# First attention of a fused two-block kernel: scores with keys on partitions, split operands, sums from a product with ones

## What is computed

```
def mla_attention(q_nope, q_rope, k_nope, k_rope, v):
    ...
        s = (jnp.einsum('bqhd,bkhd->bhqk', qn_b, k_nope, preferred_element_type=jnp.float32)
             + jnp.einsum('bqhr,bkr->bhqk', qr_b, k_rope, preferred_element_type=jnp.float32))
        p = jax.nn.softmax(s * scale, axis=-1).astype(v.dtype)
        return jnp.einsum('bhqk,bkhd->bqhd', p, v)
...
        attn_l = mla_attention(qn_l, qr_l, k_nope, k_rope, v_all)
        four_l = fourier_mix(u_f, w_fourier[l])
        y_lat = jnp.concatenate([four_l, attn_l], axis=-1) @ w_out[l]
```

## Time and profile before

| | |
|---|---|
| median of three runs | 3804.72 us |
| the profiled execution, its own time | 3807.03 us |
| its span in the profile | 3805.2 us |
| PE busy | 3570.6 us, 94% |
| DVE busy | 1533.0 us, 40% |
| ACT busy | 1040.6 us, 27% |
| the chain that ended last | PE 86%, DVE 8%, ACT 3% |

### The profile page before, as it was taken

One profiled execution on the slowest core, in us unless ns is written; L12 is line 12 of the kernel. 1 busy time (PEld: TensorE's weight loads), 2 busy tenths in 40 slices (PEclk: granted clock), 3 DMA queues, 4 the chain that ended last, 5 costly groups with the idle time before them and its releaser, 6 DMA issues.

```text
span 3805.2 us, 42399 instructions
## 1 busy us (share of the span) xinstructions
PE 3570.6 (94%) x18350; PEld 2808.2 (74%) x18350; DVE 1533.0 (40%) x2253; ACT 1040.6 (27%) x1638; POOL 0.2 (0%) x4
## 2 busy tenths in 40 slices
PE   8978999899999999899998999778788999999997
PEld 7445666687888888788886678668673678888886
DVE  4324555453122223521112764555533452333334
ACT  2033333343211111411123542332321243112122
POOL 0000000000000000000000000000000000000000
PEclk9989999899999999999998899888899999999999
DMA  7300000131111111312332000000004331111112
GB/s 288 135 16 1 1 1 1 45 119 54 50 50 45 50 50 34 133 50 78 92 97 101 20 8 18 1 17 1 1 1 160 125 97 45 50 45 56 45 45 100
DMA packets 179881, 221.14 MB, mean 58 GB/s; under 512 B 5744, under 2 KB 135408, under 8 KB 176496
## 3 DMA queue, kind: packets, MB, share of 16 engines
q1 hardware_dynamic: 179696, 218.45, 17.3%
HBM read 185.92 MB, written 32.51 MB: 57 GB/s over the span
## 4 chain that ended last, share of the span: by engine, by line
PE 86%; DVE 8%; ACT 3%; issue 1%; DMA 1%; SPq 0%; DVEq 0%; ACTq 0%
PE ps L199 83%; PE ps L809 3%; DVE M L2150 1%; DMA wr<-in_w_down 1%; PE ps L237 1%; DVE ST L890 1%; DVE X L421 0%; DVE PT L849 0%; ACT SQJ L316 0%; DVE Yf L418 0%; PE ps L1853 0%; DVE Q L1185 0%; DVE RT L1184 0%; DVE S L886 0%; DVE Y L418 0%
## 5 line engine op out<-in xcount | busy, mean ns | idle before, releaser
L373 DVE TENSOR_TENSOR wl<-wr,wh 128x1024 fp32r<-128x1024 f32 x204 | 247.2, 1224 | 602.0 <-ACT wh L365 601.9
L199 PE MATMUL ps<-hTh,wh 128*128 128x512 f32 x1216 | 474.0, 390 | 5.4 <-DVE hTl L301 2.9
L199 PE MATMUL ps<-hTl,wh 128*128 128x512 f32 x1216 | 473.6, 389 | 0.0
L199 PE MATMUL ps<-hTh,wl 128*128 128x512 f32 x1216 | 473.6, 389 | 0.0
L365 ACT ACTIVATE wh<-wr 128x1024 fp32r<-128x1024 f32 x204 | 211.9, 1053 | 728.7 <-PE ps L199 489.6
L199 PE MATMUL ps<-wh,hidh 128*128 128x512 f32 x864 | 338.0, 391 | 8.7 <-DVE wl L373 8.7
L199 PE MATMUL ps<-wl,hidh 128*128 128x512 f32 x864 | 337.7, 391 | 0.0
L199 PE MATMUL ps<-wh,hidl 128*128 128x512 f32 x864 | 337.5, 391 | 0.0
L199 PE MATMUL ps<-M,M 128*128 128x128 f32 (+1 forms) x2176 | 276.7, 288 | 4.7 <-DVE M L2150 4.7
L199 PEld LDWEIGHTS ps<-M,M 128*128 128x128 f32 (+1 forms) x2176 | 259.9, 193 | 12.1 <-DVE M L2150 6.1
L199 PEld LDWEIGHTS ps<-hTh,wh 128*128 128x128 f32 x1216 | 228.6, 188 | 53.4 <-DVE hTl L301 3.3
(11 more groups left out here) (279 smaller groups left out, 4810.5 us busy)
## 6 DMA issues: line engine op xcount, KB each, us to landing
wr<-in_w_up SPq DMA_DIRECT2D x54, 512.0 KB, 4.0
wr<-in_w_down SPq DMA_DIRECT2D x54, 512.0 KB, 3.7
wr<-in_w_in SPq DMA_DIRECT2D x42, 512.0 KB, 4.5
late<-in_w_ada SPq DMA_DIRECT2D x16, 1024.0 KB, 5.4
wr<-in_w_out SPq DMA_DIRECT2D x32, 512.0 KB, 3.7
kept<-pb SPq DMA_DIRECT2D x30, 512.0 KB, 3.1
spill<-X SPq DMA_DIRECT2D x12, 1024.0 KB, 4.0
X<-spill SPq DMA_DIRECT2D x12, 1024.0 KB, 8.7
```

Source lines behind the costliest of these rows:

```text
L199: return e.op.matmul(out, left, right, start=start, stop=stop, skip_group_check=True)
L373: e.op.tensor_tensor(lo[:, 0:k * c], self.raw[n % 3][:, 0:k * c], hi[:, 0:k * c].bitcast(F32), ALU.subtract).then_inc(*e.event(self.name + ...
```

## The change

Scores are computed transposed: 128 keys on partitions, 512 queries as columns. So the exponential's output is already what the value product needs, and the ten transposes of P for each item and their copies are gone. A step is one key tile for one half of the queries of a head: 160 steps, 20 for each head. Each step has an `mm3` for the scores (bank n % 3), one exponential of 128 x 512 to E, a copy to the f32r tile Ph, the low part Pl = E - Ph on DVE, and an `mm3` with V, which adds up ten key tiles in a bank (5 or 6). Queries, keys and values are split in high and low f32r parts as well.

The row maximum can't be taken over partitions, so the high parts alone are multiplied once more with queries on partitions (24 chunks for each head, of 512, 512 and 256 keys, through banks 3 and 4), DVE takes maxima of these, and the negated maximum becomes row 96 of the queries, against a row of ones in the keys (97 rows in the contraction). That row is made by four small products with the identity and split as well ("row"). 64 columns of ones beside V give the sums, already spread over 64 partitions; after ten steps (a "unit") ACT copies sums and values out, and for two heads at a time DVE takes the reciprocal of 128 x 512 sums and multiplies; the quotient is split straight into cath and catl.

Side jobs (`JOBS`) for the next head stand at given steps: keys at 0, 1, 2, queries at 4 and 6, values at 7 and 8, chunks two at a time from 8 to 19, row 0 at 16 and row 1 at step 1 of the head itself. All side jobs share bank 7, and each waits on PE until the one before is read out of it. The first head's jobs run before the first step (n from -20). w_q is loaded after the projection stage. `FirstOut` has no transposes of O any more.

```diff
-        e.wait_ge(("read", group))
-        e.op.tensor_copy(self.Kh[1][64:96, :], self.Kh[0][64:96, :]).then_inc(*e.event("proj_dve", "kr_both"))
...
-    SIDE, PVB = 5, 7
...
+    SIDE, MAX, VALUE, STEPS = 7, 3, 5, 160
+    KEYS = (*HALVES, (1024, 1280))
+    JOBS = {0: [("k", 0)], 1: [("k", 1)], 2: [("k", 2)], 4: [("q", 0)], 6: [("q", 1)], 7: [("v", 0)], 8: [("v", 1)], 16: [("row", 0)]}
...
+        self.Q = [pair("Q", [128, 1024], (124 + 8 * i, 128 + 8 * i)) for i in range(2)]
+        self.K = [pair("K", [128, 1280], (182 + 10 * i, 187 + 10 * i)) for i in range(2)]
+        self.V = [pair("V", [128, 10, 128], (32 + 32 * i, 48 + 32 * i)) for i in range(2)]
+        self.E = [k.sb("E", [128, 512], o) for o in (153, 172)]
+        self.P = [pair("P", [128, 512], at) for at in ((174, 180), (176, 37), (178, 53))]
...
+    def jobs(self, n):
+        h, s = n // 20 + 1, n % 20
+        out = [("row", h - 1, 1)] if s == 1 and h > 0 else []
+        if h < 8:
+            out += [(what, h, i) for what, i in self.JOBS.get(s, [])]
+            if s >= 8:
+                out += [("max", h, m // 3, m % 3) for m in (2 * (s - 8), 2 * (s - 8) + 1)]
+        return out
...
+        e.wait_ge(*[("end", "proj", n) for n in ("pe", "act", "dve")])
+        e.op.dma_start(self.wq[:, :, :], d["w_q"].rearrange("(k p) n -> p k n", p=128)).then_inc(*e.load("w_q", "w_q"))
...
+        for n in range(-20, self.STEPS):
+            if 0 <= n + 2 < self.STEPS:
+                self.score(e, n + 2)
+            for job in self.jobs(n):
+                self.max_tensor(e, job) if job[0] == "max" else self.side_tensor(e, job)
+            if n >= 0:
+                self.value(e, n)
+    def score(self, e, n):
+        h, half, kt = self.at(n)
+        if kt == 0:
+            e.wait_ge("k_rows", *[("k_low", h, i) for i in range(3)], ("q_low", h, half), ("row_low", h, half))
+        if n >= 3:
+            e.wait_ge(("exp", n - 3))
+        keys = [x[0:97, kt * 128:(kt + 1) * 128] for x in self.K[h % 2]]
+        queries = [x[0:97, half * 512:(half + 1) * 512] for x in self.Q[h % 2]]
+        mm3(e, self.bank(n % 3), keys, queries, True, True).then_inc(*e.event("att_score", ("score", n)))
+    def value(self, e, n):
+        h, half, kt = self.at(n)
+        u = n // 10
+        if kt == 0:
+            e.wait_ge("v_ones", ("v_low", h, 0), ("v_low", h, 1), ("unit_read", u - 2) if u >= 2 else None)
+        e.wait_ge(("p_low", n))
+        mm3(e, self.bank(self.VALUE + u % 2), [x[:, kt, :] for x in self.V[h % 2]], [x[:, :] for x in self.P[n % 3]], kt == 0, kt == 9).then_inc(
+            *e.event("att_value", ("value", n)))
+    def max_tensor(self, e, job):
+        _, h, t, i = job
+        m = self.chunks.index(job)
+        a, b = self.KEYS[i]
+        e.wait_ge("k_rows", *[("k_high", h, i) for i in range(3)], ("q_high", h, t // 4), ("max", *self.chunks[m - 2][1:]) if m >= 2 else None)
+        mm(e, self.bank(self.MAX + m % 2, b - a), self.Q[h % 2][0][0:96, t * 128:(t + 1) * 128], self.K[h % 2][0][0:96, a:b], True, True).then_inc(
+            *e.event("att_max", ("max_mm", h, t, i)))
...
+            e.wait_ge(("shift", h, i))
+            for t in range(4):
+                x = mm(e, self.side(t * 128, t * 128 + 128, slice(96, 97)), self.NX[:, h % 2, 4 * i + t:4 * i + t + 1], self.k.cst("ident"), True, True)
...
+        for n in range(-20, self.STEPS + 2):
+            if 0 <= n + 1 < self.STEPS:
+                self.exponential(e, n + 1)
+            for job in self.jobs(n) if n < self.STEPS else []:
+                if job[0] != "max":
+                    self.side_scalar(e, job)
+            if n % 10 == 0 and n >= 10:
+                self.unit_scalar(e, n // 10 - 1)
+            if n % 20 in (1, 11) and n // 10 % 4 in (0, 3) and n > 20:
+                self.unit_high(e, n // 10 - 1)
...
+    def exponential(self, e, n):
+        x = self.E[n % 2][:, :]
+        e.wait_ge(("score", n), ("p_low", n - 2) if n >= 2 else None)
+        e.op.activation(x, self.bank(n % 3), ACT.Exp).then_inc(*e.event("att_exp", ("exp", n)))
+        e.wait_ge(("exp", n), ("value", n - 3) if n >= 3 else None)
+        e.op.activation(self.P[n % 3][0][:, :], x, ACT.Copy).then_inc(*e.event("att_high", ("p_high", n)))
...
+            e.wait_ge(self.q_before(h, i))
+            e.op.activation(self.QT[0:64, :], self.side(rows=slice(0, 64)), ACT.Copy).then_inc(*e.event("att_act", ("q_psum", h, i)))
+            e.wait_ge(("q_psum", h, i), ("q_turned", h, i))
+            e.op.activation(self.Q[h % 2][0][0:96, s], self.QT[0:96, :], ACT.Copy).then_inc(*e.event("att_act", ("q_high", h, i)))
...
+        e.wait_ge(("value", 10 * u + 9))
+        e.op.activation(self.sums[half][rows, h // 2, :], self.bank(b, rows=sums), ACT.Copy).then_inc(*e.event("att_act", ("unit_sums", u)))
+        e.op.activation(self.raw[half][rows, h // 2, :], self.bank(b, rows=rows), ACT.Copy).then_inc(*e.event("att_act", ("unit_read", u)))
+    def unit_high(self, e, u):
+        e.wait_ge(("quotient", u))
+        e.op.activation(self.cat.half(4 + u // 4, 512 * (u % 2))[0], self.RT[:, :], ACT.Copy).then_inc(*e.event("att_act", ("high_o", u)))
...
+    def low(self, e, n):
+        hi, lo = self.P[n % 3]
+        e.wait_ge(("p_high", n))
+        e.op.tensor_tensor(lo[:, :], self.E[n % 2][:, :], hi[:, :].bitcast(F32), ALU.subtract).then_inc(*e.event("att_low", ("p_low", n)))
+    def max_vector(self, e, job):
+        _, h, t, i = job
+        a, b = self.KEYS[i]
+        e.wait_ge(("max_mm", h, t, i))
+        e.op.tensor_reduce(self.NM[:, h % 2, t, i:i + 1], self.bank(self.MAX + self.chunks.index(job) % 2, b - a), AX.X, ALU.max, negate=True).then_inc(
+            *e.event("att_dve", ("max", h, t, i)))
+        if i == 2 and t % 4 == 3:
+            s = slice(t - 3, t + 1)
+            e.wait_ge(("max", h, t, 2))
+            e.op.tensor_reduce(self.NX[:, h % 2, s], self.NM[:, h % 2, s, :], AX.X, ALU.min).then_inc(*e.event("att_dve", ("shift", h, t // 4)))
...
+            e.wait_ge(("side", *job), "rope", self.q_before(h, i))
+            e.op.tensor_tensor(R, self.side(rows=slice(96, 128)), turn[96:128, s], ALU.mult).then_inc(*e.event("att_dve", ("q_sin", h, i)))
+            e.op.tensor_tensor(Q, self.side(rows=slice(64, 96)), turn[64:96, s], ALU.mult).then_inc(*e.event("att_dve", ("q_cos", h, i)))
+            e.wait_ge(("q_cos", h, i))
+            e.op.tensor_tensor(Q, Q, R, ALU.add).then_inc(*e.event("att_dve", ("q_turned", h, i)))
+            e.wait_ge(("q_turned", h, i), ("q_high", h, i))
+            x = e.op.tensor_tensor(lo, self.QT[0:96, :], hi.bitcast(F32), ALU.subtract)
...
+    def unit_vector(self, e, u):
+        pair, half = u // 4, u % 2
+        r, o = self.sums[half][:, pair, :], self.raw[half][:, pair, :]
+        e.wait_ge(("unit_read", u))
+        e.op.reciprocal(r, r).then_inc(*e.event("att_dve", ("over_sum", u)))
+        e.wait_ge(("over_sum", u), ("q_low", min(7, u // 2 + 1), 1) if u % 2 == 0 else None)
+        e.op.tensor_tensor(self.RT[:, :], o, r, ALU.mult).then_inc(*e.event("att_dve", ("quotient", u)))
+        e.wait_ge(("high_o", u), ("quotient", u))
+        hi, lo = self.cat.half(4 + pair, 512 * half)
+        e.op.tensor_tensor(lo, self.RT[:, :], hi.bitcast(F32), ALU.subtract).then_inc(*e.event("att_dve", ("low_o", u)))
...
-        heads_tensor(self.k, e, "turn_o", self.O)
-        self.rows.tensor(e, lambda half: [("low_f", half, 3), ("read", ("turn_o", half, 3))], middle)
+        self.rows.tensor(e, lambda half: [("low_f", half, 3)], middle)
...
-            for c in range(4):
-                e.wait_ge(("mm", ("turn_o", g, c)))
-                e.op.activation(self.cat.half(4 + c, 512 * g)[0], self.k.out(("turn_o", g, c)), ACT.Copy).then_inc(*e.event("cat_act", ("high_o", g, c)))
             if g == 0:
                 self.rows.stream.scalar(e, self.rows.at + 4)
+        e.wait_ge(("low_f", 1, 3))
```

More of the change, by code:

```diff
@@ L1342, in side_jobs @@
[L1342 to L1358 removed]
+        self.k, self.p = k, p
@@ L1429, in job_vector @@
-    def job_vector(self, e, n):
-        if n is None:
-            return
-        h, part = self.jobs[n]
-        if part < 2:
-            a, b = self.part(part)
-            e.wait_ge(("side", n), self.qk_free(h), "rope", ("qr", h - 1, a) if h else None)
-            rope(e, self, None, self.Q[h % 2][64:96, a:b], a, b, "side_dve", ("qr", h, a), psum=lambda lo, hi: self.side(0, 512, slice(lo, hi)))
-    def v_copies(self, e, which):
-        for kt in range(which, 10, 2):
-            e.wait_ge(("mm", ("v", kt)))
-            copy(e, self.V[:, kt, :], self.k.out(("v", kt))).then_inc(*e.event(f"v_{e.name}", ("read", ("v", kt))))
```

210 lines of the change are left out of this document (113 added, 97 removed).

## The result

The changed kernel takes **3855.15 us** (median of four runs, 3853.08 to 3861.84) against 3806.84 for the kernel before, run beside it: a ratio of 1.0127, with a 95% interval of 1.0109 to 1.0146. It is 1.3% slower. The prediction was 3808 with a range up to 3838, so both the forecast and the range were too low, by 47 and by 17 us.

A forecast was written before the change was run, and what follows sets the result against it. TensorE was taken to bound the stage before, hand-over waits after: 323.5 + 335 + 29.5 + 37.5 + 10.5 + 6.7 = 742.7 against 727.7, +15; with -11.3 and -0.8, +2.9, so 3808 us, range 3774 to 3838.

The forecast's parts named there:

- The clock: PE's idle 4 to 5 us at divisions lowers its clock; 1.5 us lost at each, 10.5 in all.
- Steps 0 to 3: First four steps of a head, with key jobs and one row: PE 8.5 us, 11.0 with waits, one of 2.2.
- Steps 4 to 7: Next four steps, with queries and first values: PE 10.6 us, 13.2 with waits, one of 2.0.
- slower by the clock: Rival: waits inside every head drop PE's clock too, 1.8 us twice a head, 25 us more, 3833; chance 0.23.
- steps 8 to 19: Last twelve steps of a head: PE 22.3 us, DVE 21.2, taking turns as the limit; worked through, 23.7.
- The start: DVE constants, head 0's keys, queries and values, then 24 chunks, partly at low clock; first step at 323.5 us.
- R = 3.3: DVE's RECIPROCAL of 128x512 in the divisions: 3.3 us, from rows of 154 ns for one element and 160 for two.
- The rival of eight cycles an element: DVE's reciprocal takes 4.3 us for 512 elements, 8 x 1.0 more, 3816; chance 0.10.
- the end: After the last step, sums copied, reciprocal, product, high and low parts: 6.7 us; output projection 6.5 behind attention.
- The rival of a full queue: ACT and DVE far enough ahead that a head takes PE's own 41.4 us, seven times 6.5 less, 3763; chance 0.07.
- Slower: Outcome of the whole kernel over 3812 us, beyond the 0.2% a measurement tells from no change; chance 0.42.

The follow-up runs named there:

- with fillers: Changed kernel plus TensorE products nobody reads, ahead of each head's second key job and first value job and in the waits behind divisions; 3815.4 us against 3855.2.
- the fillers there: Changed kernel with unread TensorE products only before the second key job (7) and first value job (6) of each head; 3833.2 us.
- those at the divisions: Changed kernel with unread TensorE products only at the divisions' waits, 15 in step 3 of even heads, 18 in step 13 of odd heads; 3837.6 us.
- the added stalls: The three remedies plus an unread DVE reciprocal in heads 0, 2, 4, 6: 256 columns 3781.8 us, 512 columns 3797.7, 512 with seven unread PE products 3808.8.
- Ten fillers: Ten unread float32 products in the waits of the stage's first 25 us: 3808.3 us on the kernel with fillers, 3774.7 on the three remedies.
- the three remedies: Changed kernel with side jobs spaced, the quotient's copy and subtraction five steps later, and the reciprocal in four pieces of 128 columns; 3786.0 us.

## Why the prediction was wrong

The stage was forecast at 468.1 and took 515.2: 47.1 us too little. By the prediction's own steps:

| part | forecast | measured | missing |
|---|---|---|---|
| first product to first exponential | 42.4 | 46.6 | 4.2 |
| heads, apart from the clock | 402.0 | 412.8 (with fillers) | 10.8 |
| clock in the heads | 10.5 | 41.1 (453.9 - 412.8) | 30.6 |
| last step to output projection | 13.2 | 14.7 | 1.5 |

**The step that failed is "The clock".** It counted seven places, those where PE is idle 4 to 5 us, at 1.5 us each. Two things were wrong in it. First the places: the waits inside a head, which "Steps 0 to 3" and "Steps 4 to 7" had found and sized (2.2 and 2.0; measured 1.95 and 1.74 in head 1), bring the clock down as well, and the fillers there gave back 22.0 us, those at the divisions 17.6. Second the size: at a division it was 17.6 / 7 = 2.5, not 1.5 (2.3 by the stage's length). It rested on one row in which the clock was back 10 us after a wait; behind that wait stood 10.5 us of float32 products without a gap. Here PE meets its next wait soon after, and 109 of 454 us ran at the low level. The rival "slower by the clock" had the right mechanism and the right place: its 25 us come on top of the 10.5, together 35.5 for 41.1, and I gave it 0.23. The row I held against it, a clock of 1.00 over five us in which PE was half idle, was real, and the added stalls show why it is no argument: the same wait may or may not bring the clock down, so one window without a fall says little about some twenty waits.

**The heads without the clock** were each 1.0 to 1.4 us longer than worked out, 10.8 in all eight. With fillers and a full clock, steps 8 to 19 take 23.7 us in even heads, to the tenth what was worked out, and 29.5 with a division (forecast 23.7 + 6.0). Steps 0 to 7 take 25.8 in place of 24.2, and 30.4 in place of 29.05 with a division. This is not the fillers' own: head 3 of the changed kernel, which has none and whose clock stayed up until 0.6 us before step 8, takes 25.8 as well, 12.7 for steps 0 to 3 (forecast 11.0) and 13.1 for steps 4 to 7 (13.2). So the term that was too small is "Steps 0 to 3". In it ACT also copies the last unit's sums and values out (L1504, L1505, 0.59 us each), ahead of the exponential, and the working of these steps does not name them; that they are the whole difference is not shown.

**The start** was 4.2 too short. The keys were done 11.3 us after the first product, as forecast (11.4); the queries came 2.0 late, the values another 1.4 and the chunks 0.8. Ten fillers took 6.2 us out of this stretch (46.7 to 40.5, on top of the other fillers), so the clock, which this step took "for a part", is large enough for all of it.

**What held.** RECIPROCAL: R = 3.3 from two rows of one and two elements, measured in eight places:

```profile
L1590 DVE RECIPROCAL sums<-sums x8: 3333/3342/3352, 412.0 to 776.2; 128x512 f32<-128x512 f32 x8
```

(minimum, median and maximum in ns). The rival of eight cycles an element, an estimate from the repeat count of 8 in the Trainium skill ("VectorE: DVE Perf Modes", "First, the fixed hardware budget"), would be 4.3 us; the measurement decides against that reading of the page. PE's idle time at a division (for "4 to 5", 4.9 to 5.0 in odd heads; 4.15, 3.55 and 3.56 in even ones), the order of the waits, the end (6.3 for 6.5 behind it), and that the gain on PE's own work is eaten by waits: all as forecast. The rival of a full queue did not happen, and with the three remedies neither: a head takes 49.5 to 50.1 there, where PE's own work was worked out at 41.4 and DVE is busy 39 to 40.

**The chances.** Slower had 0.42, and the clock stood in two places, as a term of 10.5 us and as a rival of 25 more. They are one mechanism with a size, and its upper end could have been bounded: at the low clock f32r products start 0.43 apart in place of 0.23 (measured here), a head has 120 of them (24 us more) and some 14 us of other products that would take twice as long, so, as an estimate, up to 38 us for a head wholly at 1.2 GHz. Against such an end the range stopped far too early.

## What to carry to other kernels

Price a wait of the tensor engine as itself plus what the clock does behind it, and count every wait of about 2 us, not only the longest, though a single one may or may not bring the clock down; here, with three in a head of some 60 us, that second part came to 41 us in 454. When work is rebuilt from one engine-bound queue into many short steps that hand over between three engines, look first for long single instructions on the helpers and for jobs that share one buffer: cutting a 3.34 us reciprocal into four, taking the quotient's copy and subtraction five steps later and shifting four jobs by one step turned 1.3% slower into 0.6% faster. Products that compute nothing are a quick test whether the clock is to blame, if they stand ahead of the instruction that really waits.

## What the hardware showed that I had not expected

- At equal waits of 2.23 us the granted clock fell once in four in one kernel, and four times in four in another, in heads 2, 4 and 6 behind 90 us of the same work on PE. In the changed kernel two waits of 1.7 to 2.1 us and one of 3.6 to 5.0 in a head gave 10 to 20 us at 1.2 GHz.
- The reciprocal of 128 partitions costs by the column: 3.34 us for 512 and 0.94 for 128, so 0.14 us and 6.25 ns for each column, which fits the 1.74 of 256 columns too; a plain operation of 512 columns takes 0.69 in all.
- The same code ahead of the stage brought the stage's first product at 272.8 to 281.8 us in different profiles, a scatter as large as some of the effects measured here. It follows the time at 1.2 GHz in those stages, 13.7 to 41.0 us. Only the stage's own length, and medians of several runs, tell such effects apart.
